# A hybrid decoder layer on eight cores: state reloads placed later, the second half's recurrence started later, and one gate product moved from GpSimd to VectorE

## What is computed

```python
x = x + 0.5 * swiglu(rmsnorm(x, g_ffn1), w_ffn1_in, w_ffn1_out)      # (silu(gate) * up) @ w_out
h = rmsnorm(x, g_mix)
u_a, v_a, q_b, k_b, v_b, g_b, lr_b, gate_a, gate_b = jnp.split(h @ w_in, IN_SPLITS, axis=-1)
# mixer A: spatial gating of chunks of 128 positions -> y_a
# mixer B: per 4 heads, S_t = diag(a_t) S_{t-1} + k_t^T v_t, o_t = q_t S_t, block by block
o, s_new = gla_recurrence(q, k, v, log_a, s0, gla_block)
y_b = rmsnorm(o, g_gla_out) * jax.nn.silu(g_b)
mix = jax.nn.sigmoid(gate_a) * (y_a @ w_proj_a) + jax.nn.sigmoid(gate_b) * (y_b @ w_proj_b)
x = x + mix @ w_out
x = x + 0.5 * swiglu(rmsnorm(x, g_ffn2), w_ffn2_in, w_ffn2_out)
x = x + (p @ w_ple) * jax.nn.sigmoid(rmsnorm(x, g_ple) @ w_ple_gate)
```

## Time and profile before

| | us |
|---|---|
| median of 3 runs | 1592.76 (1590.1 to 1597.75) |
| the profiled execution, its own time | 1595.69 |
| span of its slowest core (7) | 1594.1 |
| spans of the eight cores | 1576.1 to 1594.1 |
| TensorE busy on core 7 | 1519.3 |
| VectorE, ScalarE, GpSimd busy | 916.9, 642.4, 333.0 |

### The profile page before, as it was taken

How to read it: one execution, slowest core, us unless ns; L and a number is a source line. 1 busy time by engine, 2 the same in 40 slices (tenths; PEclk the granted TensorE clock), 3 DMA queues, 4 the chain that set the end, 5 groups by cost and what they waited for, 6 DMA issues and landing times.

```text
span 1594.1 us, 27407 instructions; the slowest of 8 cores (1576.1 to 1594.1 us)
## 1 busy us (share of the span) xinstructions
PE 1519.3 (95%) x10818; PEld 1018.6 (64%) x10818; DVE 916.9 (58%) x1731; ACT 642.4 (40%) x1256; POOL 333.0 (21%) x434
## 2 busy tenths in 40 slices
PE   6999999999799999997998999999999998999996
PEld 4588775655574688853457885444454557888755
DVE  5577337647644855743697773466266376454256
ACT  4243214634633545421355342236456234442135
POOL 3023201101131023310223341011012201232027
PEclk9999999999899999998999999999999999999999
DMA  9659979673937357996746797653423422457413
GB/s 196 90 119 176 159 126 160 101 140 87 169 82 158 120 165 171 205 195 154 175 119 163 161 189 143 151 114 56 77 47 73 100 70 72 160 121 135 77 28 108
DMA packets 74693, 203.82 MB, mean 128 GB/s; under 512 B 8321, under 2 KB 28434, under 8 KB 69444
## 3 DMA queue, kind: packets, MB, share of 16 engines
q0 software_dynamic: 29232, 100.73, 40.2%
q1 hardware_dynamic: 44916, 100.78, 19.6%
q10 hardware_dynamic: 416, 0.55, 0.2%
HBM read 258.36 MB, written 41.25 MB: 188 GB/s over the span
## 4 chain that ended last, share of the span: by engine, by line
PE 80%; DMA 7%; DVE 5%; issue 3%; ACT 3%; POOL 1%; DVEq 0%; SPq 0%; POOLq 0%; ACTq 0%
PE ps L43 41%; PE ps L399 38%; DMA s_ring<-w_ffn_in 3%; DMA s_x<-x 2%; DMA s_tmp<-x 1%; ACT L480 1%; ACT s_tmp L480 1%; DMA s_s<-x 1%; DVE s_ar L490 1%; DVE s_ar L502 1%; DVE s_xn L502 1%; POOL s_ring L510 1%; DVE s_x L502 0%; DVE s_ring L490 0%; DVE s_Sf L502 0%
## 5 line engine op out<-in xcount | busy, mean ns | idle before, releaser
L399 PE MATMUL ps<-s_xn,s_ring 128*128 128x256 bf16 (+3 forms) x2204 | 382.6, 301 | 0.0
L399 PE MATMUL ps<-s_ar,s_ring 128*128 128x512 bf16 (+2 forms) x1963 | 380.5, 337 | 0.0
L43 PE MATMUL ps<-s_xn,s_ring 128*128 128x256 bf16 (+3 forms) x2084 | 356.6, 298 | 19.1 <-ACT s_tmp L480 5.3
L399 PEld LDWEIGHTS ps<-s_ar,s_ring 128*128 128x128 bf16 x1963 | 190.7, 98 | 143.9 <-issue 4.5
L399 PEld LDWEIGHTS ps<-s_xn,s_ring 128*128 128x128 bf16 x2204 | 215.6, 98 | 82.4 <-issue 0.4
L43 PEld LDWEIGHTS ps<-s_xn,s_ring 128*128 128x128 bf16 x2084 | 201.6, 98 | 97.0 <-ACT s_tmp L480 8.0
L480 ACT ACTIVATE s_tmp<-ps 128x512 f32<-128x512 f32 (+3 forms) x344 | 172.1, 511 | 204.7 <-PE ps L399 164.9
L43 PE MATMUL ps<-s_ar,s_ring 128*128 128x512 bf16 (+2 forms) x1077 | 213.1, 328 | 7.9 <-ACT s_tmp L480 2.8
L43 PE MATMUL ps<-s_xs,s_ring 128*128 128x256 bf16 (+1 forms) x1388 | 204.9, 274 | 2.5 <-ACT ps L480 2.1
L493 POOL TENSOR_TENSOR s_ar<-s_tmp 128x256 bf16<-128x256 f32 (+1 forms) x160 | 125.7, 806 | 370.3 <-DVE s_tmp L490 364.6
L480 ACT ACTIVATE s_sq<-s_x 128x512 bf16<-128x512 f32 (+2 forms) x138 | 81.7, 605 | 209.1 <-DVE s_x L502 197.9
(11 more groups left out here) (167 smaller groups left out, 1404.2 us busy)
## 6 DMA issues: line engine op xcount, KB each, us to landing
s_ring<-sums SPq DMA_DIRECT2D x41, 896.0 KB, 6.1
s_ring<-w_in POOLq DMA_DIRECT2D x24, 1024.0 KB, 12.1
s_ring<-w_ffn_out POOLq DMA_DIRECT2D x32, 704.0 KB, 9.7
s_ring<-w_ffn_in POOLq DMA_DIRECT2D x39, 512.0 KB, 10.9
sums<-s_ring SPq DMA_DIRECT2D x11, 896.0 KB, 9.6
s_s<-st SPq DMA_DIRECT2D x16, 512.0 KB, 6.5
ss_out<-s_s SPq DMA_DIRECT2D x16, 512.0 KB, 6.3
y<-s_x SPq DMA_DIRECT2D x32, 256.0 KB, 3.0
```

The costliest lines, as they stand in the source:

```text
L43: ins = self._e.matmul(*a, **k)
L399: ins = e.matmul(o, l, r, start=s, stop=t, skip_group_check=shared)
```

## The change

Four edits, all in the code that builds the program:

```diff
-def diagonal(v, r, n):
-
-    a = v(r, n, n)
+def diagonal(v, r, n, main=False):
+
+    a = v(r, 0 if main else n, n)
     (p, np_), (one, m) = a.ap
-    return bass.AP(a.tensor, a.offset, [[p, np_], [v.cols - n, 2], [one, m]])
+    return bass.AP(a.tensor, a.offset, [[p, np_], [v.cols + (n if main else -n), 2], [one, m]])
...
                 g, h, j = S.g[1], S.a["h"], self.j
+                if True:
+                    K.tt(diagonal(h, j, n, True), split2(g.wide(0, 0, 2 * n)), split2(tw(0, 0, 2 * n)), ALU.mult,
+                         [g.wide.k(0, 0, 2 * n), tk], [h.k(j, 0, n), h.k(j + 1, n, n)])
+                    tmps.free(g)
+                    tmps.free(t)
+                    return
                 for r, c0 in ((j, 0), (j + 1, n)):
                     K.ptt(h(r, c0, n), g.wide(0, c0, n), tw(0, c0, n), ALU.mult, [g.wide.k(0, c0, n), tw.k(0, c0, n)], [h.k(r, c0, n)])
...
-                K.dma("sp", ss_d[n_].rearrange("h k v -> k h v"), s0.ap, f"s0s{n_ % 2}", reads=[s0.k()], nbytes=524288)
+                st_ = K.dma("sp", ss_d[n_].rearrange("h k v -> k h v"), s0.ap, f"s0s{n_ % 2}", reads=[s0.k()], nbytes=524288)
...
                 if n_ + 2 < NS:
-                    yield 0.6 * SPACE
+                    yield max(0.6 * SPACE, p.ops[st_]["t1"] + 3500.0 - K.now)
                     load_s0(n_ + 2)
...
-                S.rec = K.spawn(rec(S))
+                S.rec = K.spawn(rec(S), 14000.0 if S.X else 0.0)
...
-                        yield K.until(t.k(), margin=4000.0)
+                        yield K.until(t.k(), margin=6000.0)
```

## The result

| | before | after |
|---|---|---|
| median of the runs | 1591.94 us | 1575.97 us |
| the profiled execution, its own time | 1595.69 | 1578.89 |
| spans of the eight cores | 1576.1 to 1594.1 | 1557.7 to 1577.3 |

The change is faster: the ratio of after to before is 0.9888, 95% interval 0.9852 to 0.9925, that is 17.8 us of 1592 (11.9 to 23.6). One of the runs after (1647 us) had the cores of one die at a lower clock; it is in the median above, but not in the ratio. Against 1576 us predicted the time is as forecast. What follows shows that two of the terms behind it were not.

A forecast was written before the change was run, and what follows sets the result against it. TensorE's own work was taken as the bound, leaving its idle and low-clock time to win. Terms summed to -20.4 us on core 7 (1575.3) and -12.7 on core 3 (1576.4); the slower gave 1576 us, range 1563 to 1589.

The forecast's parts named there:

- Recurrence: Mixer, second half's recurrence delayed into m60 and m61: -7.3 us in the first pair, -1.3 in the second.
- Gate product: FFN stretches, 80 VectorE products replace 160 on GpSimd: +1.5 us of added waiting in the first stretch.
- -1.6 for fillers: Around the samples, 67 filler matmuls instead of 81, 0.116 us each: -1.6 us; 0 if their waits remain.
- State and x pieces: FFN 2's second product, first pair: -10.7 us on core 7, -3.0 on core 3; stretch behind it -1.0.
- the sums 684 and 418 ns: Sign of being right: VectorE's weight sums become shorter than 788 and 609 ns.
- m4 to m61 at 59 us or less: Sign of being right: first pair's mixer stretch m4, m60, m61, 64.6 us before, at 59 or less.
- No wait over 4 us for a state: Sign of being right: TensorE has no wait over 4 us for a sample's state.
- The first (the state wait moves): SP queue: stores still hold reloads, core 7 keeps 9 of its 10.7 us; 1584 to 1585 us, chance 0.12.
- The third: Four FFN stretches: VectorE becomes the bound; 1617 us if all of the 43 us net show; chance 0.06.
- The second: Mixer: recurrence ends too late, m4 of the second half waits; no 7.3 us gain, 1586 us, chance 0.10.
- The fourth: Nothing lasting: idle time comes back at the next wait for the same late transfers; 1592 us, chance 0.06.

## Why the prediction was right

The time came out as forecast with one of the three large terms right and two wrong. That the sum fits is luck: on the core that decided the forecast, 3, the gate product and the fillers brought 5.6 us where 0.1 stood, and the state and x pieces nothing measurable where 4.0 stood, so the errors nearly cancel.

- **Recurrence**, -8.6 predicted for both pairs: right in sign and place, and in size within the interval (8.6 alone, 6.0 to 11.0; 4.4 + 1.5 in the stages themselves). Half of the 8.3 us idle is 4.15, not the 4.3 of the sum. What stays in m60 is 3 to 8 us of idle time, up to 3.8 of it for weights. I had kept the other half for chains without naming this transfer, whose 18 us from issue to use were covered only because m60 used to start later.
- **Gate product**, +1.5 predicted: the step that failed is "I add as much waiting as there is" in the first stretch and nothing elsewhere. The first stretch came as said in number (+1.8), and VectorE's load too (55.7 for 55.4). But the load is not the whole reason there: with twice the products the stretch takes 116.4 us, less than the 117.3 with one, and the order of its last units is that of before again. What the removed GpSimd product held back was not costed: the start of FFN 1's second product in the second pair (-3.0, shown above), FFN 2's first product (-2.9, with 22 fillers fewer), and the order of the state queue. Measured -5.6 alone. That also holds the -1.6 for fillers: the 14 fewer fillers are this edit's. Their price is that of the waits under them where there are any; at the place with 24 of them some 1.1 us lay over no wait.
- **State and x pieces**, -10.7 and -1.0 predicted: the mechanism is there, the term was mis-sized. The 11.0 us of core 7 were one core's wait in one execution; on the other cores with complete records it was 2.6 to 4.2. The 9 to 16 us that I took for loads are landings of stores. Alone the edits gave 4.6, and beside the gate product nothing that can be measured. I read the new order of the SP and VectorE queues in the changed kernel as their doing; the gate product edit alone moves them as well, and the x piece ahead of the first store is its doing.
- **What would show it**: GpSimd 205.5 us (207 said), the product 0.692 us, the sums 684 and 418 ns, the first stretch 117.3 on most cores: right. m4 to m61 at 59 us or less: on three of the six cores with complete records, and 62.3 on core 5. No wait over 4 us for a state: wrong on core 5, 6.4.
- **Rivals.** The first (the state wait moves) happened on core 5 in one profile and in none of four others of all edits, but again on two cores with the product twice (6.5 and 7.2 us). The third is out: twice the product costs 4 to 7 us. The second sets in between 14 and 22 us of delay. The fourth holds in part: late transfers, of weights or of a state, still stand in the profiles of the cores that end last (core 5 after, core 3 without the state edits).

## What to carry to other kernels

When the program fills expected waits with dummy matmuls, busy TensorE time hides the waits: look for fillers first, and read from the time line what the matmul behind them needs and when that ended, because a filler can also be longer than its wait. Before costing an instruction that moves to another engine, ask who waits for the old one at the ends of a stretch, not only what the new one adds, and compare the order of work that the planner then makes. And a wait that is long on one core in one execution is no term of the sum: take its size from several cores, and test edits together, because two that re-sort the same queue may pay once.

## What the runs showed of the hardware

Three weight sums took 2.68 us beside two GpSimd products, which took 1.97 in place of 1.41 (the rows at 654.57 and 654.73 above). By themselves the sums take 1.63 us:

```profile
150.93 1.63 DVE L490 TENSOR_TENSOR s_ring<-s_ring 128x1024 bf16<-128x1024 bf16 x3 [1.93 <-DMA s_ring<-w_ffn_in]
152.48 0.68 DVE L490 TENSOR_TENSOR s_tmp<-ps,s_ar 128x512 f32<-128x512 f32 x1
...
153.22 1.06 PE L43 MATMUL ps<-s_xn,s_ring 128*128 128x264 bf16 x4 [2.53 <-DVE s_tmp L490]
```

The Trainium skill, SBUF — State Buffer, "Who interferes with whom", calls the port pair that the two share an exclusive lock. The trace agrees, one instruction at a time. The first sum starts first and takes 0.68 us, as by itself; the first product, begun beside it, takes 1.10 for 0.72; the second sum, begun beside that, 0.95 for 0.42; the second product 0.90; the last sum 1.21 for 0.69. Each ends 0.3 to 0.6 us behind the end of the other engine's instruction before it. The whole, 2.68 us, is less than the 1.63 + 1.41 one after the other, because an instruction's start overlaps the end of the one that it waits for (my reading of these times). The rows just shown (core 5 after, first stretch) also show the other cost of a fixed order: VectorE stands 1.93 us for a late piece of weights, the add that a matmul needs is queued behind the sums, and TensorE stands 2.53 us. And the cores differ more than I had thought: in one execution of the same program, for an undisturbed 1544.0 us, the last embedding ended at 1548.3 us on core 0 and at 1564.8 on core 5.
